# Sixteen column units of a projection multiplied as plain fp32, with the retention states loaded later

## The reference, cut to what matters

```python
z = rmsnorm(x, norm_g) @ w_in                       # (264, 1024) @ (1024, 3584)
qa, ka, va, qb, kb, vb, gb = jnp.split(z, AB_SPLITS, axis=-1)   # seven parts of 512
qa, ka = rope(qa), rope(ka)
oa = moba_attend(qa, pos, k_all, v_all)             # samples read 1024 cached keys and values each
qb, kb = rope(qb), rope(kb) * DK_B ** -0.5
ob, s_new = retention(qb, kb, vb, s0, chunk)        # samples start from state_ret
y = concat(oa, head_rmsnorm(ob) * silu(gb)) @ w_out
```

## Time and profile before

| | |
|---|---|
| median of 3 runs | 962.98 us (961.5 to 964.55) |
| profiled execution: span from first to last instruction | 959.2 us |
| its own device time | not listed apart from the three runs; the median is 3.8 us above the span |
| PE busy | 883.4 us (92%) |
| DVE, ACT, POOL busy | 622.1, 420.1, 257.4 us |
| mean granted TensorE clock | 0.923 of 2.4 GHz |
| first projection | about 23.8 to 146.2 us |
| attention and retention of the prompt | about 147 to 202 us |

### The profile page before, as it was taken

The page is one execution under the profiler, slowest core; times in us unless marked ns, Lnnn a source line. Parts: engine busy times, 40 slices in busy tenths (PEclk is TensorE's granted clock), DMA queues, the critical chain, the costliest instruction groups (busy, mean ns, idle before and its releaser), DMA issues.

```text
span 959.2 us, 16875 instructions
## 1 busy us (share of the span) xinstructions
PE 883.4 (92%) x6145; PEld 761.0 (79%) x6145; DVE 622.1 (65%) x943; ACT 420.1 (44%) x695; POOL 257.4 (27%) x226
## 2 busy tenths in 40 slices
PE   2999894969999999999999999969969999999996
PEld 1988783742325999999999999857648999999995
DVE  3689988660032798888556656565476888887442
ACT  4434333341011565555545433564334655555442
POOL 6154767710100332232001000161221332222010
PEclk9999996588999999999999999975597999999997
DMA  9837675335565555554556667403353566653631
GB/s 275 284 129 242 199 260 183 128 94 160 192 220 175 176 177 175 178 184 129 172 177 192 191 187 216 161 10 100 88 155 93 171 192 188 188 157 121 183 119 46
DMA packets 154406, 159.83 MB, mean 167 GB/s; under 512 B 11793, under 2 KB 136349, under 8 KB 154335
## 3 DMA queue, kind: packets, MB, share of 16 engines
q1 hardware_dynamic: 145520, 151.09, 50.6%
q10 hardware_dynamic: 7966, 6.33, 2.2%
q0 software_dynamic: 864, 1.68, 0.7%
HBM read 150.76 MB, written 8.50 MB: 166 GB/s over the span
## 4 chain that ended last, share of the span: by engine, by line
PE 81%; DVE 11%; ACT 4%; issue 2%; DMA 2%; ACTq 0%; POOL 0%; SPq 0%; DVEq 0%
PE bank L1396 20%; PE bank L1397 20%; PE bank L1398 20%; PE bank L1604 6%; DVE w_lo L921 3%; DVE sc_all L973 2%; PE bank L1773 1%; PE bank L1726 1%; DMA z<-in_c_out_norm_g 1%; PE bank L1485 1%; PE bank L1600 1%; PE bank L1566 1%; PE bank L1748 1%; PE bank L1737 1%; DVE z L968 1%
## 5 line engine op out<-in xcount | busy, mean ns | idle before, releaser
L530 ACT ACTIVATE w_hi<-w_raw 128x1024 fp32r<-128x1024 f32 (+2 forms) x230 | 227.9, 993 | 297.8 <-PE bank L1398 294.5
L921 DVE TENSOR_TENSOR w_lo<-w_raw,w_hi 128x1024 fp32r<-128x1024 f32 (+2 forms) x230 | 296.1, 1289 | 83.6 <-ACT w_hi L530 83.4
L1396 PE MATMUL bank<-actB_hi,w_hi 128*128 128x264 f32 x704 | 200.1, 284 | 0.0
L1397 PE MATMUL bank<-actB_lo,w_hi 128*128 128x264 f32 x704 | 199.5, 283 | 0.0
L1398 PE MATMUL bank<-actB_hi,w_lo 128*128 128x264 f32 x704 | 199.3, 283 | 0.0
L1396 PE MATMUL bank<-actA_hi,w_hi 128*128 128x264 f32 x624 | 184.8, 296 | 5.8 <-DVE w_lo L921 2.9
L1397 PE MATMUL bank<-actA_lo,w_hi 128*128 128x264 f32 x624 | 180.1, 289 | 0.0
L1398 PE MATMUL bank<-actA_hi,w_lo 128*128 128x264 f32 x624 | 179.8, 288 | 0.0
L1397 PEld LDWEIGHTS bank<-actB_lo,w_hi 128*128 128x128 f32 x704 | 132.6, 188 | 0.1
L1396 PEld LDWEIGHTS bank<-actB_hi,w_hi 128*128 128x128 f32 x704 | 132.6, 188 | 0.1
L1398 PEld LDWEIGHTS bank<-actB_hi,w_lo 128*128 128x128 f32 x704 | 132.0, 187 | 0.0
(11 more groups left out here) (326 smaller groups left out, 1191.2 us busy)
## 6 DMA issues: line engine op xcount, KB each, us to landing
w_raw<-in_ffn_w SPq DMA_DIRECT2D x44, 1024.0 KB, 5.3
kv<-in_cache_k SPq DMA_DIRECT2D x64, 256.0 KB, 3.0
kv<-in_cache_v SPq DMA_DIRECT2D x64, 256.0 KB, 3.1
w_raw<-in_c_w_in SPq DMA_DIRECT2D x16, 1024.0 KB, 5.6
w_raw<-in_ab_w_in SPq DMA_DIRECT2D x14, 1024.0 KB, 5.4
w_raw<-in_ffn_w SPq DMA_DIRECT2D x16, 768.0 KB, 4.5
w_raw<-in_ffn_w SPq DMA_DIRECT2D x16, 640.0 KB, 4.1
w_raw<-in_ab_w_out SPq DMA_DIRECT2D x4, 1024.0 KB, 5.7
```

Source lines behind the costliest of these rows:

```text
L530: A(whi[u % RING][:, 0:nk, :], raw[u // 2 % RING][:, 0:nk, P * (u % 2):P * (u % 2) + P], ACT.Copy).then_inc(sem("hi_ready"), 1)
L921: V.tensor_tensor(wlo[u % RING][:, 0:nk, :], raw[u // 2 % RING][:, 0:nk, P * (u % 2):P * (u % 2) + P], whi[u % RING][:, 0:nk, :].bitcast(F ...
L1396: M(bank[b][:, 0:T], hi[:, k, :], src[0][:, k0 + k, :], start=first and k == 0, stop=False)
L1397: M(bank[b][:, 0:T], hi[:, k, :], src[1][:, k0 + k, :], start=False, stop=False)
```

## The change

Units 12 to 27 are no longer split. PE multiplies the raw fp32 weights by unsplit fp32 activations, 8 matmuls a unit. ACT makes these activations (`plain`) once, after the first norm's seed. They lie in the buffer of `s0` (seven tiles) and in `ptt[0]` (one), so the states are loaded only behind unit 27: POOL waits for `mm_done` 28 and issues them behind its loop. A raw buffer that held units 12 to 27 is freed by their matmuls (`mm_done`), no longer by their split. `n_split(u)` counts the split units up to u. Three semaphores of POOL's memsets became one.

```diff
+PLAIN = range(12, 28)
+def n_split(u):
+    return u + 1 - min(max(u + 1 - PLAIN.start, 0), len(PLAIN))
...
+        s0f = s0[:, :, :, :].rearrange("p c b e -> p (c b e)")
+        plain = [s0f[:, T * k:T * k + T] for k in range(7)] + [ptt[0][:, 0:T]]
...
             def load_raw(r, src, i8=0):
                 if r >= RING:
-                    sp.wait_ge(sem("lo_ready"), 2 * (r - RING) + 2 + i8)
+                    u = 2 * (r - RING) + 1
+                    if u in PLAIN:
+                        sp.wait_ge(sem("mm_done"), u + 1)
+                    else:
+                        sp.wait_ge(sem("lo_ready"), n_split(u) + i8)
...
-            for b in range(NB):
-                pool.dma_start(s0[:, :, b, :], state_ret[0, b].rearrange("(c q) d e -> (q d) c e", q=2)
-                               ).then_inc(sem("s0_landed"), 16)
...
                 if u >= 8:
                     k_mult(u - 8)
+            pool.wait_ge(sem("mm_done"), PLAIN.stop)
+            for b in range(NB):
+                pool.dma_start(s0[:, :, b, :], state_ret[0, b].rearrange("(c q) d e -> (q d) c e", q=2)
+                               ).then_inc(sem("s0_landed"), 16)
             for j in range(20, 32):
                 k_mult(j)
...
             def split_hi(u, i8=0):
-                if u >= U_END:
+                if u >= U_END or u in PLAIN:
                     return
...
             rsqrt_seed("rms", 1, var[:], nwt[:], rstd[:])
+            for k in range(KT):
+                A(plain[k], x[:, k, :], ACT.Copy, scale=gains[:, G_AB + k:G_AB + k + 1]).then_inc(sem("norm_plain"), 1)
...
             def split_lo(u, i8=0):
-                if u >= U_END:
+                if u >= U_END or u in PLAIN:
                     return
-                dve.wait_ge(sem("hi_ready"), u + 1 + i8)
+                dve.wait_ge(sem("hi_ready"), n_split(u) + i8)
...
+            def plain_unit(u, b):
+                pe.wait_ge(sem(f"w_landed{u // 2 % RING}"), 16 * (u // 8 + 1))
+                pe.wait_ge(sem("norm_plain"), KT)
+                for k in range(KT):
+                    ins = M(bank[b][:, 0:T], raw[u // 2 % RING][:, k, P * (u % 2):P * (u % 2) + P], plain[k], start=k == 0, stop=k == KT - 1)
+                ins.then_inc(sem("mm_done"), 1)
...
             for u in range(28):
                 claim(u % RING, "evac_done", u + 1)
-                unit(u, u % RING, actA, ready=("norm_lo", 0) if u == 0 else None)
+                if u in PLAIN:
+                    plain_unit(u, u % RING)
+                else:
+                    unit(u, u % RING, actA, ready=("norm_lo", 0) if u == 0 else None)
```

More of the change, by code:

```diff
@@ L333, in _ @@
             ffn_loads(0, U_UP0, U_DN0)
-            sp.wait_ge(sem("lo_ready"), U_IN1 - 2 * RING + 2)
+            sp.wait_ge(sem("lo_ready"), n_split(U_IN1 - 2 * RING + 1))
             with nc.allow_non_contiguous_dma(reason="16 columns of gates"):
@@ L368, in _ @@
             G = nc.gpsimd
-            G.memset(ones[:], 1.0).then_inc(sem("ones_ready"), 1)
+            G.memset(ones[:], 1.0).then_inc(sem("pool_set"), 1)
             pool.dma_start(pg[:], page_table.rearrange("(o b) n -> o (b n)", o=1)).then_inc(sem("pages_landed"), 16)
@@ L437, in ffn_pool @@
                 for s in range(4):
-                    G.memset(ffa[s][:, 0:2], 0.0).then_inc(sem("pad_zero"), 1)
+                    G.memset(ffa[s][:, 0:2], 0.0).then_inc(sem("pool_set"), 1)
                 def group(f, i4, fd):
@@ L459, in _ @@
             pool.wait_ge(sem("c_small"), 64)
-            G.memset(sel[:], 0.0).then_inc(sem("sel_ready"), 1)
-            pool.wait_ge(sem("sel_ready"), 1)
-            G.memset(sel[:, H - 1:H], 1.0).then_inc(sem("sel_ready"), 1)
+            G.memset(sel[:], 0.0).then_inc(sem("pool_set"), 1)
+            pool.wait_ge(sem("pool_set"), 6)
+            G.memset(sel[:, H - 1:H], 1.0).then_inc(sem("pool_set"), 1)
             pool.wait_ge(sem("small_out"), 2)
@@ L739, in conv_rows_out @@
                         act.dma_start(o.rearrange("t (f p) -> t f p", p=P), rows).then_inc(sem("stored"), 16)
-                act.wait_ge(sem("pad_zero"), 4 + 4 * l)
+                act.wait_ge(sem("pool_set"), 5 + 6 * l)
                 group(0, u_up, 0, 0, 0, True)
@@ L1388, in unit @@
             def unit(u, b, src, k0=0, nk=8, first=True, last=True, i8=0, ready=None):
-                pe.wait_ge(sem("lo_ready"), u + 1 + i8)
+                pe.wait_ge(sem("lo_ready"), n_split(u) + i8)
                 hi, lo = whi[u % RING], wlo[u % RING]
@@ L1419, in _ @@
                 TR(bank[k % 4][:, TP:T], xs_tok[:, P * k:P * k + P], ident[0:NB, 0:NB]).then_inc(sem("x_t"), 1)
-            pe.wait_ge(sem("ones_ready"), 1)
+            pe.wait_ge(sem("pool_set"), 1)
             def job(n):
@@ L1782, in _ @@
             pe.wait_ge(sem("jobs_out"), len(JOBS) + len(JOBS1))
-            pe.wait_ge(sem("sel_ready"), 2)
+            pe.wait_ge(sem("pool_set"), 7)
             claim(7, "h1_var", 1)
```

## The result

| | before | changed |
|---|---|---|
| median | 962.51 us (6 runs, 955.29 to 964.73) | 991.84 us (6 runs, 990.49 to 998.59) |
| ratio | | 1.0329, 95% interval 1.0288 to 1.0369 |
| profiled execution: device time, span | 961.5, 959.2 us | 998.59, 996.8 us |
| mean granted TensorE clock | 0.923 | 0.906 |

The change makes the kernel slower by 29.3 us. The profiled execution of the changed kernel is the longest of its six runs, 7 us above the median, so times summed up from its rows come out a few us longer than the medians show.

What follows compares the result with a forecast made beforehand. It took PE to set the end almost everywhere, with DVE full at 96 to 108 us; after the change, PE and page waits. +16.7 (late `k_sum(20)`) - 1.5 (front) + 3 (clock) = +18 on 963 gave 981 us, range 966 to 997.

Steps and rivals of the forecast that it cites:

- PE's price: In the projection, a plain unit takes PE 3.56 us, 0.65 us more than a split one, 10.4 us over 16 units.
- In the best case the two nearly cancel: At the projection's end, PE's added time and DVE's freed time offset: 146.5 us if nothing else bound, against 146.2 before.
- ACT's copies: At the start, eight copies make PE about 1.6 us later until unit 8; with DVE's relief net 0, bounds 0 to +1.6.
- The front: Before the first matmul, small loads land earlier without the states' 1 MB: 1.5 us gained, from a possible 0 to 3.
- The clock, one plain unit: Behind PE's new stops in the projection, one plain unit runs at 1.2 GHz: 3 us more, bounds 0 and 14.
- Pages 6.8 us after the raw load: On SP's queue, a raw load's first page pair lands 6.8 us after the raw load's issue, bounds 2.7 to 9.
- The 16.7 us go through.: In the attention, `k_sum(20)` comes 16.7 us later and later products don't bind again, so the whole delay reaches the end.
- The clock falls further: Rival: four or more plain units run at 1.2 GHz, costing 14 us instead of 3; 992 us, chance 0.17.
- The pages hardly matter: Rival: pages land 3 us after issue and the states hide behind heads 0 and 1; 963 to 966 us, chance 0.08.
- the attention swallows part: Rival: PE and ACT work ahead on heads 1 and 2 while DVE waits, regaining 7 us; 974 us, chance 0.13.
- The faster case: Rival: small loads land 3 us earlier, DVE's relief gives 1.5 before unit 12, pages arrive in time; 958.7 us, chance 0.06.
- The states' 6 us: On POOL between pair 19 and `k_mult(20)`, the eight state DMAs take 6.03 us, formerly where POOL had nothing else to do.

Runs made afterwards that it cites:

- experiment 1: The changed kernel with each raw DMA from raw 10 on issued behind its two page pairs instead of ahead of them; 966.75 us, ratio 1.0057.
- experiment 3: The kernel before, all units split, with raw DMAs 10 to 17 waiting for the freeing unit's multiplication instead of its split; 989.36 us, ratio 1.0276.
- experiment 5: The changed kernel with ACT's eight plain copies spread one each over turns 1 to 8 of its unit loop; 993.74 us, ratio 1.0296.
- experiment 9: The changed kernel with ACT's stores of prompt and sample keys and values moved behind its attention loop; 992.4 us, ratio 1.0299.
- experiment 10: The changed kernel with SP's register loads of page numbers ahead of the wait of the group's raw DMA; 993.64 us, ratio 1.0302.
- experiment 4: The kernel before with only the eight state DMAs moved from the head of POOL's list to ahead of `k_mult(20)`; 963.08 us, ratio 1.0018.
- experiment 2: The changed kernel with POOL's eight state DMAs issued behind `k_mult(31)` instead of ahead of `k_mult(20)`; 988.78 us, ratio 1.028.
- experiment 6: The changed kernel with pages ahead of raw loads, states behind `k_mult(31)` and ACT's copies spread, all together; 960.99 us, ratio 0.9958.
- experiment 11: The changed kernel with page pairs issued ahead of the raw DMA for raw 10 to 13 only; 989.69 us, ratio 1.0287.
- experiment 8: The edits of experiment 6 with only units 12 to 19 plain, units 20 to 27 split as before; 960.65 us, ratio 0.9965.

## Why the prediction was right, and where it was short

**Direction and mechanism: right.** 981 was forecast, within 966 to 997; 991.84 was measured, so the loss was 29 us where 18 were forecast. The step named as the cause, pages on SP behind a raw load that now waits for PE, is shown by experiments 1 and 3 from both sides. The signs it named came, most of them larger: POOL waited 9.9, 2.5, 9.0 and 12.8 us at pairs 4, 10, 14 and 18, where 4 to 9 was forecast.

**PE's price: exact.** A plain unit in the timeline of PE, unit 12:

```profile
79.59 3.28 PE L1419 MATMUL bank<-s,w_raw 128*128 128x264 f32 x14
82.71 0.61 PE L1419 MATMUL bank<-ptt,w_raw 128*128 128x264 f32 x2
83.15 1.05 PE L1419 MATMUL bank<-s,w_raw 128*128 128x264 f32 x4
```

83.15 - 79.59 = 3.56 us, as taken from the sum of squares. "In the best case the two nearly cancel" also holds: with the wait out of the way unit 27 is evacuated at 148.1 to 149.3, against 146.5 forecast and 146.18 before.

**The chain, step by step.** PE's end of a unit is the issue of its raw load:

| step | predicted | measured | short by |
|---|---|---|---|
| unit 13 ends | 84.3 | 86.9 | 2.6 |
| unit 19 | 112.1 | 116.2 | 4.1 |
| unit 21 | 121.2 | 125.7 | 4.5 |
| unit 23 | 134.2 | 140.65 | 6.4 |
| unit 27 | 156.3 | 163.8 | 7.5 |
| product 18 begins | 163.1 | 173.1 | 10.0 |
| product 20 ends | 176.3 | 186.2 | 9.9 |

The steps that failed are sizes:

- *ACT's copies, "net 0, bounds 0 to +1.6".* Measured +3.1 us, outside the bounds, all by unit 2. In the timelines of ACT and PE:

```profile
33.57 2.95 ACT L573 ACTIVATE s<-x,gains 128x264 f32<-128x264 f32 x7
36.41 0.51 ACT L573 ACTIVATE ptt<-x,gains 128x264 f32<-128x264 f32 x1
```

```profile
38.17 1.25 PE L1487 MATMUL bank<-z,cst 128*128 128x264 f32 x2 [2.21 <-ACT convp L595]
38.85 0.80 PE L1409 MATMUL bank<-actA_hi,w_hi 128*128 128x264 f32 x1
39.44 0.42 PE L1410 MATMUL bank<-actA_lo,w_hi 128*128 128x264 f32 x1
39.66 0.42 PE L1411 MATMUL bank<-actA_hi,w_lo 128*128 128x264 f32 x1
```

The first split behind the seed starts at 36.82, 3.5 us late (33.34 in the earlier trace rows), much as forecast. The swap waits 2.2 us for the eviction behind it and comes at 38.17, where it was 36.66: 1.5 us late, as forecast. What was left out is the clock: behind that stop PE's split products start 0.22 us apart, not 0.12, and the granted clock is 0.54 from 38 to 40 us and 0.61 from 40 to 42, where the kernel before and experiment 5 have 1.00. Experiment 5 takes 3.3 us back at unit 2. By unit 11 the delay is 2.5 us (79.79 against 77.26), so 0.5 was given back.

- *The front, 1.5 us.* The first matmul came at 13.82, about 0.2 us earlier than before (13.99), and by the sum of squares (28.55 against 28.32) this was gone. So the small loads were not held up by the states' megabyte by more than this.
- *Between the units.* From the end of unit 13 to the end of unit 21 the chain had 36.9 us, 28.5 of them for eight units, and so 8.4 for the swaps, query broadcasts and turns between them. In the starts of L1419 these took 10.3.
- *The clock, one plain unit.* Two came: units 22 and 26 took 4.90 and 4.37 us for 14 records, in place of 3.28, each behind one of the stops of PE that the prediction had placed (waits of 3.02 and 4.06 us). The granted clock was 0.57 from 130 to 134 us and 0.59 from 156 to 158. Together this cost 2.7 us, just the 3 of the sum. The Trainium skill (TensorE: Matmul & The Clock Gate, "HAM oscillation") would have each stop put PE back; the trace agrees for these two, and one unit later the pace is 3.56 again.

```profile
128.65 1.06 PE L1459 MATMUL bank<-cst,z 128*128 128x128 f32 x8 [3.02 <-DVE z L981]
129.96 0.71 PE L1461 MATMUL bank<-cst,z 128*8 128x128 f32 x4 [0.25 <-ACT tok_kb L586]
130.47 4.90 PE L1419 MATMUL bank<-s,w_raw 128*128 128x264 f32 x14
```

- *Pages 6.8 us after the raw load.* Right at six of eight places (6.2 to 7.0), 7.6 at raw 10 and 9.3 at raw 17, where ACT's stores of 1 MB ran beside them (experiment 9: 6.6 without). That is the 2.5 us at product 18. The register load that the prediction did not see on SP cost nothing that the runs can tell (experiment 10).
- *"The 16.7 us go through."* At `k_sum(20)` the forecast was 18.2 us with the front and the clock, and 26.6 came. The copies (2.6), the front (1.3), the work between the units (1.9) and the landing of the last pages (2.5) are nearly all of the difference. At the attention end it was 35.3, so 8.6 more were lost in the attention, where the prediction had nothing. Some 4.6 of them go with the row of 6.81 us shown above: DVE's small operation of head 3 is held until POOL has done its six products. Experiment 4 has the same row with nothing but the states moved, and takes 4.6 us more than the kernel before from `k_sum(20)` to the attention end. In experiment 2, where that operation takes 0.22, the stretch is 46.1 us and in the changed kernel 51.5. Between 140 and 240 us PE waited 19.0 us for the attention's weights (three waits on `ptt`) where it was 4.7, and 6.1 for `smx` where it was 9.6. From `k_sum(20)` to the attention end its mean granted clock was 0.53, before 0.63. The rest may come from this, but no run takes it apart.
- *From the profiled execution to the median.* From the attention end to the end of the device time, a stretch that the edits hardly touch, the 14 profiled executions took 755.2 to 760.9 us, so several us between any two of them are scatter. The two profiled executions differ by 37.1 us (998.59 against 961.5), the medians by 29.3, since that of the changed kernel was 7 us above its median. How much of the 35.3 at the attention end belongs to that scatter is not known.

**The rivals.** "The clock falls further", 992, gives the right number by the wrong way: two slow plain units in the projection, not four, and 2.7 us in place of 14. "The pages hardly matter" falls with experiment 3, "the attention swallows part" with the row of `k_sum(20)` and what follows it: the attention added to the loss. The faster case asked for pages landed when POOL asks; experiments 1 and 6 come near to it (POOL waits 25.1 us for pages in experiment 1, 20.1 before the change). With the pages alone turned round the kernel is still no faster than before (1.0057). With states and copies moved too it gains some 0.4%, barely clear of none, and the front has no part in that.

**The states' 6 us.** As a term it was right in size (6.06), and product 20 ends 6 us later for it (experiment 2: 5.1 us earlier, with unit 27 1.1 later). The longer hold on DVE came with it, too (experiment 4). Yet its worth in the medians is small: 3 us in experiment 2, and nothing to tell in experiment 4.

## What to carry to other kernels

When a buffer's release moves from an early engine to a late one, look at the queue that issues its load: the load itself may have all the time it needs, and what stands behind it has not. Put what is due sooner ahead of the load that waits: here this took back 25 of 29 us, and with the states and copies moved as well the edit that cost 3% cost nothing. A wait costs most where nothing else is left to do beside it, which here was the end of the stage.

## What the runs showed of the hardware that was not expected

- DVE's `TENSOR_SCALAR` on 128x2 elements takes 0.17 us in most places where POOL is not multiplying. When POOL multiplied 128x1024 (2.3 us), it mostly lasted until the product under way was over: 0.91 to 2.16 us in the kernel before, 2.22 in experiment 2. In the changed kernel it took 6.81 us, until POOL's row of six products ended at 197.62. `TENSOR_REDUCE` beside the same products kept its 1.2 us. The Trainium skill (SBUF — State Buffer, "Who interferes with whom") says that `tensor_scalar` can take ports that DVE shares with GpSimd, that whoever issues first keeps them for its whole instruction while the other is blocked, and that `tensor_reduce` never contends. The trace agrees for `TENSOR_REDUCE` and for the 2.2 us beside one product of 2.3. But 6.81 spans three products, which that rule does not give. The row is 6.80 or 6.81 in six kernels (the changed one, experiments 4, 5, 9, 10 and 11), and these are the ones where product 20 starts right behind the states' DMAs and opens six products without a gap. In experiment 6 the operation starts at the same place, just behind the start of the fourth of six products without a gap (7.05 us after product 20 began, 7.06 in the changed kernel), but no such DMA stands ahead of them:

```profile
164.16 2.24 DVE L1018 TENSOR_SCALAR sm<-sm 128x2 f32<-128x2 f32 x1
```

  Experiments 2, 3 and 8 are like it (2.22 to 2.23). So the DMAs ahead and the six products without a gap were both there each time, and how they make the hold longer was not tried.
- In the changed kernel POOL could start on the first pair 6.2 to 7.0 us after the raw load's issue (1.5 MB in all) at six of eight places, whether the pages were issued 0.6 or 3.2 us behind the raw load.
- In 14 profiled executions the stretch from the first result of the first ConvFFN (`ffa<-bank,rstd` on DVE) to the end of the device time took 620.8 to 621.0 us in ten, 619.2 in two and 625.7 and 626.3 in two, one of these the kernel before. Between the attention end and that result it took 132.8 us in the kernel before and 140.0 in the changed one. So two executions can differ by 5 us and more in stretches that the edits leave as they are, and one trace of each cannot settle a difference of that size.
